# Loading the first token tile of x through two DMA queues in a one-core decoder-block kernel

## The chip, the cores and the metric

One core of a Trainium2 chip runs the whole kernel. The metric is the device time of one execution in microseconds (us). The engines named here are PE (TensorE, matrix products), ACT (ScalarE), DVE (VectorE), POOL (GpSimd) and SP (SyncE, which here only issues DMAs). Two engines issue DMAs in this kernel: SP on the queue that the profile calls q1, and ScalarE on the queue that it calls q10. "SPq" and "ACTq" are the instruction queues of those two engines.

## The reference, cut to what matters

```
ada = c @ w_ada + b_ada;  shift, scale, gate = split(ada, 3)
h   = rms_norm(x, g_pre) * (1 + scale) + shift        # x: 256 x 2048, float32
proj = h @ w_in                                       # then two attention branches,
...                                                   # their gates, a merge and w_out
x   = x + gate * rms_norm(y, g_post)
```

The change touches only the first lines: x and the small vectors (c, b_ada, g_pre, g_kv, g_subln) are read from HBM. Everything later is as it was.

## The kernel before, in words

x has 256 tokens, kept as two token tiles of 128 (one token to a partition) in `x_tok[:, t, :]`, 1 MB each. The matrix products want h with the model dimension on the partitions, so the opening turns x on PE. It also needs the modulation (shift and scale), which comes out of a product of the vector c with the first 4096 columns of w_ada. The opening goes so:

- **SP's queue.** L516 issues x tile 0, then tile 1, each with its own semaphore `x_in[t]`. Then L526 issues the sixteen halves of the first ada group (`load_ada(0, q)`, q from 0 to 7, 256 KB each, 4 MB in all) and L572 the first 512 KB weight piece (`w_raw`). After that weight pieces and later ada groups alternate in an order that is written out by hand.
- **ScalarE.** L971 and L974 issue five small DMAs that put the vectors into the rows of one tile, `vec_rows` (69 rows of 512 bytes), all on the semaphore `vec_in`. Then, per token tile, L979 squares x and sums it (waiting for `x_in[t]`). Then it copies the turned x out of PSUM (L983), casts the first weight piece (L1036) and makes the first h from turned x, gain and shift (L992). An activation table is loaded ahead of the first square.
- **POOL** makes the identity (L609, L611) and turns each sum of squares into 1/rms (L633, L636).
- **DVE** waits for the turned vectors, copies them out of PSUM into `cols` (L1541), makes small products of them (L1543, L1544, L1551), multiplies the identity by 1/rms of tile 0 (`make_diag(0)`, L1538), and then adds up the ada rows: two instructions for each q (L1435 for q = 0, L1438 after it), fifteen in all, since one of the sixteen parts is left to PE. `make_diag(1)` stands behind q = 1. At the end L1448 and L1449 make shift and gain for the first h.
- **PE** first runs four products whose results nobody reads (`keep_clock(6, 4)`, L1643). It waits for all five vector DMAs and turns `vec_rows` (L1814). It waits for `x_in[t]` and the diagonal of tile t and turns x in eight groups of four products, of which each shows as two instructions (L1823, 64 in all: groups 0 to 3 are tile 0, groups 4 to 7 are tile 1). After two more unread products (`keep_clock(1, 2)`) it sums the ada rows over the partitions in three sets (L1634): the odd rows, the part left to PE, the even rows. Then the first weight piece follows (L1899, L1913) and the stream of products that fills the rest of the kernel.

The order on each engine is the order in which its block is written, and each engine runs strictly by it; semaphores alone tie them together. A wait for one DMA is a wait for 16, since a DMA counts its semaphore up by 16.

Of the kernel before, what the change touches and what calls it, by code (L numbers as in the profile page):

```python
# [34 lines left out]
P = 128  # L35
D = 2048
SEQ = 256
TOK = SEQ // P
# [92 lines left out]
def hybrid_block(nc, x, c, positions, w_ada, b_ada, g_pre, w_in, g_kv, w_ukv,  # L131
# [78 lines left out]
    with ExitStack() as ctx:  # L210
# [8 lines left out]
        def sb(name, shape, dt, offset=None):  # L219
            size = 4 if dt != BF16 else 2  # L220
            for s in shape[1:]:
                size *= s
            if offset is None:
                offset = room((size + 31) // 32 * 32)
            return nc.alloc_sbuf_tensor_at(name, shape, dt, offset=offset)
# [22 lines left out]
        x_tok = sb("x_tok", [P, TOK, D], F32, r_o_lo)  # L248
# [96 lines left out]
        def sem(name):  # L345
            return ctx.enter_context(nc.semaphore(name))
# [5 lines left out]
        x_in = [sem(f"x_in{t}") for t in range(TOK)]  # L352
# [159 lines left out]

        @block.sync
        def _(sp):
            for t in range(TOK):
                sp.dma_start(x_tok[:, t, :], x[0, t * P:(t + 1) * P, :]).then_inc(x_in[t], 16)  # L516
            def load_ada(j, q):

                n = j * (KT // 2) + q
                if n >= ADA_RING:  # L520
                    sp.wait_ge(ada_used, n - ADA_RING + 1)
                if j == 1 and (q, 1) in FIRST_ON_PE:
                    sp.wait_ge(ada_direct, 1)
                for s in range(2):
                    col = s * D + j * 2 * P
                    sp.dma_start(ada_slot(n)[:, :, s, :],  # L526
                                 w_ada[0, 2 * q * P:2 * (q + 1) * P, col:col + 2 * P]
                                 .rearrange("(t p) n -> p t n", p=P)).then_inc(ada_in[n % ADA_RING], 16)
# [48 lines left out]
            for p, (a, kind, n, i, first, last) in enumerate(pieces):  # L577
# [18 lines left out]
                if kind == "wout" and n >= 1 and i % 2 == 0 and n < 3:  # L596
                    part = (n - 1) * 4 + i // 2
                    t, half = part // 4, slice(part % 4 * CH, (part % 4 + 1) * CH)
# [327 lines left out]
        for h in range(HEADS):  # L926
            s, t, v, g = mla_at[h]
# [3 lines left out]
            s, t, v, g = diff_at[h]  # L931
# [36 lines left out]

        @block.scalar
        def _(eng):  # L970
            eng.dma_start(vec_rows[V_C:V_C + KT, :], c[0, :].rearrange("(r n) -> r n", n=P)).then_inc(vec_in, 16)  # L971
            for row, n, v in ((V_SHIFT, 2 * KT, b_ada[0, 0:2 * D]), (V_GPRE, KT, g_pre[0, :]),
                              (V_GKV, RANK // P, g_kv[0, :]), (V_GSUB, 1, g_subln[0, :])):
                eng.dma_start(vec_rows[row:row + n, :], v.rearrange("(r n) -> r n", n=P)).then_inc(vec_in, 16)  # L974
            for t in range(TOK):
                eng.wait_ge(x_in[t], 16)
                if t:
                    eng.wait_ge(x_sq, t)
                act.activation(sq_junk[:, :], x_tok[:, t, :], ACT.Square, accum_out=sumsq[:, R_X, t:t + 1]).then_inc(x_sq, 1)  # L979
            for g in range(KT // 2):  # L980
                eng.wait_ge(xT_made, g + 1)
                t, k = g // 4, g % 4 * 4
# [388 lines left out]
        for h in range(HEADS):  # L1371
            s, t, v, g = mla_at[h]
# [4 lines left out]
            s, t, v, g = diff_at[h]  # L1377
            dve_after[g + 4].append(dve_o_lo(HEADS + h))
            dve_after[v + 4].append(head_squares(h))
        for h in range(HEADS):  # L1380
            s, t, v, g = diff_at[h]
# [229 lines left out]
        def _(pe):  # L1611
# [204 lines left out]
            for g in range(KT // 2):  # L1816
                t, k = g // 4, g % 4 * 4
                bank = g
                if g % 4 == 0:
                    pe.wait_ge(x_in[t], 16)  # L1820
                    pe.wait_ge(diag_ready, t + 1)
                for b in range(4):
                    ins = mm(ps[:, bank, b * P:(b + 1) * P], lhsT=x_tok[:, t, (k + b) * P:(k + b + 1) * P],  # L1823
                             rhs=x_diag[:, t, :], start=True, stop=True)
                ins.then_inc(xT_made, 1)
# [154 lines left out]
```

## Time and profile before

| | |
|---|---|
| median of three runs | 765.11 us (764.71 to 765.16) |
| the profiled execution, its own time | 764.76 us |
| its span in the trace | 763.0 us |
| PE busy in the span | 752.8 us |
| DVE, ACT busy | 560.3 us, 424.3 us |
| moved by DMA | 189.71 MB, mean 249 GB/s |

The span is what the trace records, from the first instruction to the last; the execution's own time is 1.8 us longer. A timeline row reads: start, duration, engine, line, operation, the tile written and the tile read, shapes, count, and in square brackets how long the engine was idle before and what ended that idle time. Consecutive instructions of one kind are merged into one row.

### The profile page before, as it was taken

How to read it: one execution, taken by the hardware profiler on the slowest of the kernel's cores; microseconds unless marked ns; L12 is line 12 of the kernel's file. 1: busy time of each engine (PE TensorE's matmuls, PEld its weight loads, DVE VectorE, ACT ScalarE, POOL GpSimd, SP SyncE). 2: the span in 40 equal slices, each digit the busy share in tenths (PEclk: the TensorE clock that was granted, in tenths of full speed). 3: DMA queues.
4: the chain of work that ended last, by engine and by line, in shares of the span. 5: the costliest groups of instructions: out<-in, count | busy, mean ns of one | idle time of the engine just before them, and what ended most of it. 6: DMA issues, size and time to landing. Idle time of an engine off the chain costs nothing.

```text
span 763.0 us, 10086 instructions
## 1 busy us (share of the span) xinstructions
PE 752.8 (99%) x3681; PEld 625.1 (82%) x3681; DVE 560.3 (73%) x823; ACT 424.3 (56%) x618; POOL 22.2 (3%) x95
## 2 busy tenths in 40 slices
PE   7999999999999999999999999999999999999997
PEld 5778888888888988888888888888888888888885
DVE  4899998888779579888987768776554556465554
ACT  5689777767656554544545664655444444444441
POOL 2000000000000000000000000011100000000001
PEclk9999999999999999999999999999999999999999
DMA  9999999999584788888886575555556656567642
GB/s 338 395 393 395 357 378 375 339 375 314 172 246 127 219 277 303 290 284 275 295 287 191 163 216 179 168 167 165 187 172 196 191 184 201 186 207 248 221 160 110
DMA packets 132555, 189.71 MB, mean 249 GB/s; under 512 B 10325, under 2 KB 68122, under 8 KB 132250
## 3 DMA queue, kind: packets, MB, share of 16 engines
q1 hardware_dynamic: 132240, 188.77, 74.0%
q8 instruction: 29, 0.48, 0.2%
q10 hardware_dynamic: 266, 0.30, 0.1%
q14 instruction: 20, 0.16, 0.1%
HBM read 185.90 MB, written 2.10 MB: 246 GB/s over the span
## 4 chain that ended last, share of the span: by engine, by line
PE 96%; SPq 2%; DMA 1%; ACT 1%; DVE 0%; issue 0%; DVEq 0%; ACTq 0%
PE ps L1923 17%; PE ps L1925 17%; PE ps L1924 17%; PE ps L1913 16%; PE ps L1899 8%; PE ps L1882 8%; PE ps L1885 4%; SPq L526 2%; PE ps L1718 1%; DMA w_raw<-in_w_in 1%; PE ps L1703 1%; PE ps L1733 1%; PE ps L1876 1%; PE ps L1875 1%; PE ps L1873 1%; PE ps L1692 0%
## 5 line engine op out<-in xcount | busy, mean ns | idle before, releaser
L1569 DVE TENSOR_TENSOR w_both<-w_raw,w_both 128x1024 fp32r<-128x1024 f32 x248 | 301.9, 1222 | 160.6 <-ACT w_both L1036 159.1
L1036 ACT CAST w_both<-w_raw 128x1024 fp32r<-128x1024 f32 x248 | 258.9, 1050 | 239.4 <-PE ps L1925 183.0
L1913 PE MATMUL ps<-w_both,h_both 128*128 128x512 f32 x560 | 138.5, 389 | 0.0
L1913 PEld LDWEIGHTS ps<-w_both,h_both 128*128 128x128 f32 x560 | 105.1, 188 | 22.2
L1923 PE MATMUL ps<-w_both,h_both 128*128 128x512 f32 x296 | 116.8, 395 | 0.0
L1925 PE MATMUL ps<-w_both,h_both 128*128 128x512 f32 x296 | 115.4, 390 | 0.0
L1924 PE MATMUL ps<-w_both,h_both 128*128 128x512 f32 x296 | 115.2, 389 | 0.0
L1899 PE MATMUL ps<-w_both,h_both 128*128 128x512 f32 x280 | 76.0, 393 | 1.0 <-ACT h_both L992 0.7
L1314 DVE SCALAR_TENSOR_TENSOR ada_acc<-ada_ring,cols,ada_acc 128x512 f32<-128x512 f32 x98 | 69.6, 745 | 0.5
L1923 PEld LDWEIGHTS ps<-w_both,h_both 128*128 128x128 f32 x296 | 55.6, 188 | 12.7 <-issue 1.7
L1925 PEld LDWEIGHTS ps<-w_both,h_both 128*128 128x128 f32 x296 | 55.6, 188 | 11.7
L1882 PE MATMUL ps<-h_both,w_both 128*128 128x512 f32 x256 | 64.9, 395 | 0.0
L1924 PEld LDWEIGHTS ps<-w_both,h_both 128*128 128x128 f32 x296 | 55.6, 188 | 11.0
L1899 PEld LDWEIGHTS ps<-w_both,h_both 128*128 128x128 f32 x280 | 51.7, 188 | 12.3 <-issue 1.0
L1882 PEld LDWEIGHTS ps<-h_both,w_both 128*128 128x128 f32 x256 | 46.1, 189 | 9.7 <-issue 1.3
L1923 PE MATMUL ps<-w_both,o_hi 128*128 128x512 f32 x128 | 50.2, 392 | 0.0
L1925 PE MATMUL ps<-w_both,o_lo 128*128 128x512 f32 x128 | 49.8, 389 | 0.0
L1924 PE MATMUL ps<-w_both,o_hi 128*128 128x512 f32 x128 | 49.8, 389 | 0.0
L1314 DVE SCALAR_TENSOR_TENSOR ada_acc<-gate_ring,cols,ada_acc 128x512 f32<-128x512 f32 x60 | 44.8, 747 | 2.1 <-DMA gate_ring<-in_w_ada 1.1
L1923 PE MATMUL ps<-w_both,m_hi 128*128 128x512 f32 x116 | 45.2, 390 | 0.0
L1925 PE MATMUL ps<-w_both,m_lo 128*128 128x512 f32 x116 | 45.2, 389 | 0.0
L1924 PE MATMUL ps<-w_both,m_hi 128*128 128x512 f32 x116 | 45.1, 389 | 0.0
(266 smaller groups left out, 849.3 us busy)
## 6 DMA issues: line engine op xcount, KB each, us to landing
w_raw<-in_w_in SPq DMA_DIRECT2D x177, 512.0 KB, 4.5
ada_ring<-in_w_ada SPq DMA_DIRECT2D x128, 256.0 KB, 6.8
gate_ring<-in_w_ada SPq DMA_DIRECT2D x32, 512.0 KB, 5.1
w_raw<-in_w_out SPq DMA_DIRECT2D x32, 512.0 KB, 3.8
w_raw<-in_w_o_mla SPq DMA_DIRECT2D x16, 512.0 KB, 3.7
w_raw<-in_w_o_diff SPq DMA_DIRECT2D x16, 512.0 KB, 4.1
w_raw<-in_w_ukv SPq DMA_DIRECT2D x16, 256.0 KB, 3.4
x_tok<-in_x SPq DMA_DIRECT2D x2, 1024.0 KB, 6.4
```

Of the source, the lines that this page charges most:

```text
L526: sp.dma_start(ada_slot(n)[:, :, s, :], w_ada[0, 2 * q * P:2 * (q + 1) * P, col:col + 2 * P] .rearrange("(t p) n -> p t n", p=P)).then_inc ...
L1036: act.copy(w_hi[:, p % RING, :], w_raw[:, p % RING, :]).then_inc(hi_done, 1)
L1314: ins = dve.scalar_tensor_tensor(out=acc, in0=src, scalar=cc, in1=acc, op0=ALU.mult, op1=ALU.add)
L1569: dve.tensor_tensor(w_lo[:, p % RING, :], w_raw[:, p % RING, :], w_hi[:, p % RING, :].bitcast(F32), ALU.subtract).then_inc(lo_done, 1)
L1703: mm(ps[:, 4 + w, lo:lo + keys], lhsT=qnT[:, 2 * u + w, t * P:(t + 1) * P], rhs=knT[:, 2 * u + w, 0:keys], start=t == 0, stop=False, skip_ ...
L1882: mm(ps[:, b0 + c, :], lhsT=w_hi[:, p % RING, (2 * r + c) * P:(2 * r + c + 1) * P], rhs=h_both[:, :, 4 * i + r, :], start=first and r == 0 ...
L1885: ins = mm(ps[:, b0 + c, 0:SEQ], lhsT=w_lo[:, p % RING, (2 * r + c) * P:(2 * r + c + 1) * P], rhs=h_hi[:, 4 * i + r, :], start=False, stop ...
L1899: mm(ps[:, b0 + t, :], lhsT=h_hi[:, 2 * i + r, t * P:(t + 1) * P], rhs=w_hi[:, p % RING, r * CH:(r + 1) * CH], start=fresh and r == 0, sto ...
L1913: ins = mm(ps[:, b0 + t, :], lhsT=side[:, 2 * i + r, t * P:(t + 1) * P], rhs=w[:, p % RING, r * CH:(r + 1) * CH], start=False, stop=last a ...
L1923: mm(o, lhsT=s_hi[:, k, q], rhs=hi, start=fresh and r == 0, stop=False, skip_group_check=kind == "early")
L1924: mm(o, lhsT=s_hi[:, k, q], rhs=lo, start=False, stop=False, skip_group_check=kind == "early")
L1925: ins = mm(o, lhsT=s_lo[:, k, q], rhs=hi, start=False, stop=last and r == tiles - 1, skip_group_check=kind == "early")
```

## The change

Tile 0 of x is loaded as two DMAs of 64 rows (512 KB each). Partitions 0 to 63 stay on SP's queue. Partitions 64 to 127 become the first DMA of ScalarE's queue, ahead of the five vector DMAs. Tile 1 stays on SP's queue, behind the first half of tile 0. The two places that wait for tile 0 (ScalarE's square and PE's turning) now wait for 32 on `x_in[0]`, and still for 16 on `x_in[1]`.

```diff
         @block.sync
         def _(sp):
-            for t in range(TOK):
-                sp.dma_start(x_tok[:, t, :], x[0, t * P:(t + 1) * P, :]).then_inc(x_in[t], 16)
+            sp.dma_start(x_tok[0:P // 2, 0, :], x[0, 0:P // 2, :]).then_inc(x_in[0], 16)
+            sp.dma_start(x_tok[:, 1, :], x[0, P:TOK * P, :]).then_inc(x_in[1], 16)
...
         @block.scalar
         def _(eng):
+            eng.dma_start(x_tok[P // 2:P, 0, :], x[0, P // 2:P, :]).then_inc(x_in[0], 16)
             eng.dma_start(vec_rows[V_C:V_C + KT, :], c[0, :].rearrange("(r n) -> r n", n=P)).then_inc(vec_in, 16)
...
             for t in range(TOK):
-                eng.wait_ge(x_in[t], 16)
+                eng.wait_ge(x_in[t], 16 * (2 - t))
...
                 if g % 4 == 0:
-                    pe.wait_ge(x_in[t], 16)
+                    pe.wait_ge(x_in[t], 16 * (2 - t))
                     pe.wait_ge(diag_ready, t + 1)
```

## Rows read from the trace of the kernel before

**Rows 1.** The page of the profile: span, PE's share, chain that ended last.

```profile
span 763.0 us, 10086 instructions
PE 752.8 (99%) x3681; PEld 625.1 (82%) x3681; DVE 560.3 (73%) x823; ACT 424.3 (56%) x618; POOL 22.2 (3%) x95
PE 96%; SPq 2%; DMA 1%; ACT 1%; DVE 0%; issue 0%; DVEq 0%; ACTq 0%
```

**Rows 2.** Waits of PE after the opening (24 to 764 us): total, times, longest.

```profile
PE ps L1954 <- ACT x_diag L1051: 1.1, 1, 1.1
PE ps L1899 <- ACT sum_junk L1005: 0.3, 1, 0.3
```

**Rows 3.** Timeline of PE's products, 1 to 24 us (start, duration, what).

```profile
1.51 5.60 PE L1643 MATMUL ps<-ident 128*128 128x512 f32 x8 [1.51 <-POOL ident L611]
8.57 0.25 PE L1814 MATMUL ps<-ident,vec_rows 69*128 69x69 f32 x1 [1.46 <-DMA vec_rows<-in_g_subln]
9.71 7.38 PE L1823 MATMUL ps<-x_diag,x_tok 128*128 128x128 f32 x64 [0.88 <-DVE x_diag L1538]
16.93 1.88 PE L1643 MATMUL ps<-ident 128*128 128x512 f32 x4
19.10 1.16 PE L1634 MATMUL ps<-ones,ada_acc 128*128 128x128 f32 x8 [0.29 <-DVE ada_acc L1438]
20.99 1.05 PE L1634 MATMUL ps<-ones,ada_acc 128*128 128x128 f32 x8
22.76 1.17 PE L1899 MATMUL ps<-w_both,h_both 128*128 128x512 f32 x4 [0.71 <-ACT h_both L992]
```

**Rows 4.** Timeline of the other engines, 0 to 32 us.

```profile
6.05 1.91 ACT L979 ACTIVATE sq_junk<-x_tok 128x2048 f32<-128x2048 f32 x1 [1.24 <-DMA x_tok<-in_x]
8.49 0.56 POOL L636 TENSOR_TENSOR rstd<-variance,power 128x1 f32<-128x1 f32 x1
8.65 1.91 ACT L979 ACTIVATE sq_junk<-x_tok 128x2048 f32<-128x2048 f32 x1 [0.60 <-DMA x_tok<-in_x]
...
8.86 0.23 DVE L1541 COPY cols<-ps 128x69 f32<-128x69 f32 x1 [8.86 <-PE ps L1814]
...
9.28 0.28 DVE L1538 TENSOR_SCALAR x_diag<-ident,rstd 128x128 f32<-128x128 f32 x1
9.48 0.17 DVE L1551 TENSOR_SCALAR cols<-cols 128x28 f32<-128x28 f32 x1
...
9.99 0.88 DVE L1435 TENSOR_SCALAR ada_acc<-ada_ring,cols 128x512 f32<-128x512 f32 x2 [0.34 <-DMA ada_ring<-in_w_ada]
...
11.40 1.45 DVE L1438 SCALAR_TENSOR_TENSOR ada_acc<-ada_ring,cols,ada_acc 128x512 f32<-128x512 f32 x2 [0.53 <-DMA ada_ring<-in_w_ada]
...
13.00 7.56 DVE L1438 SCALAR_TENSOR_TENSOR ada_acc<-ada_ring,cols,ada_acc 128x512 f32<-128x512 f32 x11
...
20.91 1.04 ACT L1036 CAST w_both<-w_raw 128x1024 fp32r<-128x1024 f32 x1 [3.19 <-DMA w_raw<-in_w_in]
...
22.01 1.09 ACT L992 ACTIVATE h_both<-xnT,mod_shift,mod_gain 128x256 fp32r<-128x256 f32 x2
```

**Rows 5.** The same timeline: issues on SPq and ACTq, and the table load.

```profile
0.72 0.86 SPq L516 DMA_DIRECT2D x_tok<-in_x  x2
...
2.11 1.13 ACTq L974 DMA_DIRECT2D vec_rows<-in_g_kv  x1
...
3.27 0.23 ACTq L974 DMA_DIRECT2D vec_rows<-in_g_subln  x1
...
3.53 1.28 ACT L979 ACT_TABLE_LOAD   x1 [3.53 <-issue]
```

**Rows 6.** DMA, 0 to 40 us: GB/s in each of 40 slices of 1 us.

```profile
GB/s 0 66 135 389 393 413 430 386 371 376 383 384 383 384 384 382 385 383 397 404 381 405 394 385 393 383 397 404 385 404 393 391 406 384 398 401 385 405 390 390
```

**Rows 7.** DMA, q10's packets at 0 to 4 us, then at 4 to 8 us.

```profile
q10 hardware_dynamic: 32, 0.01, 1.9%
...
q10 hardware_dynamic: 90, 0.03, 2.8%
```

**Rows 8.** Stretch 0 to 5 us: busy, PE clock, DMA share, GB/s (order of columns: PE PEld DVE ACT POOL).

```profile
0.00:5.00 5.00, 3.49 (x4) 1.50 (x5) 0.00 (x0) 1.28 (x1) 2.24 (x43) 1.00 0.54 197
```

## The prediction

> **What bounds the kernel now.** I began with the page. PE is busy for 752.8 of 763.0 us and the chain that ended last is 96% PE [rows 1]. So the end moves only by what moves PE's stream of products. The list of PE's waits after 24 us shows two: 0.3 us for the gain sums and 1.1 us for a diagonal at the very end [rows 2]. From the first product on a weight piece, at 22.76 us [rows 3], there is therefore next to nothing that could swallow a shift: whatever this change gains or loses, it gains or loses as a shift of that 22.76 us, about one for one. All that matters is what sets that moment.
>
> **What sets 22.76 us.** The timeline shows three paths that meet there, and the reader should see how near to each other they are.
>
> Path A, the weight piece. It lands just before the cast at 20.91 us; the cast ends at 21.95 and the first h starts at 22.01 [rows 4]. It is queued behind 2 MB of x and 4 MB of ada, and from 3 us on the DMA moves 370 to 430 GB/s without a gap [rows 6]. So path A is a matter of total bytes and of how early full rate is reached. ScalarE had idled 3.19 us ahead of the cast.
>
> Path B, the ada sums on DVE. It starts at 9.99 us, after 0.34 us of waiting for the first ada part, waits 0.53 us for the second, and from 13.00 us adds eleven times in 7.56 us, 0.69 us each, with no idle time of note [rows 4]. It lets PE start its three sets of sums at 19.10 us, after 0.29 us of idle time [rows 3].
>
> Path C, PE itself. It turns x from 9.71 us on, runs the unread products from 16.93 to 18.81, and from 19.10 the three sets of sums, of which the last ends at 22.04 (20.99 + 1.05) [rows 3]. Path C starts with the diagonal at 9.28 us, which stands on DVE behind the vector columns (8.86 us), which stand behind PE's turning of the vectors at 8.57, which waited 1.46 us for the last vector DMA [rows 3, 4].
>
> So paths B and C meet at PE's sums: B sets their start, and C has 0.29 us to spare against it. Path A meets them at the first h and has 0.06 us to spare, since the cast ends at 21.95.
>
> **The change, part by part.**
>
> Tile 0 of x. It must land before the square at 6.05 us [rows 4]. The same 1 MB goes over, now from two queues. Between 0 and 5 us the row of slices adds up to 66 + 135 + 389 + 393, or 0.98 MB [rows 6], about one tile, and the square starts a microsecond after that. At full rate one queue keeps the DMA engines busy, so a second queue can only help in the slow slices, 1 to 3 us. I take no gain. The bounds are 0 and the time that full rate in those two slices would give back: they moved 0.20 MB where 390 GB/s would have moved 0.78, so 0.58 MB or 1.5 us at most, and nothing suggests all of it. Even then the square's result is not what path C waits for: 1/rms of tile 0 is there at 9.05 (8.49 + 0.56), but DVE has the vector columns only at 9.09 (8.86 + 0.23) [rows 4]. An earlier tile 0 alone is worth nothing.
>
> That is the place to weigh a rule. The Trainium skill, page "DMA: Bandwidth & Descriptors", section "Rules for kernel authors", advises against two transfers to disjoint partition halves, because both halves run over the same 16 engines, whether issued from one engine or two. By it tile 0 lands when it did and the start stays. The trace bears it out above 3 us, where one queue already reaches 389 to 430 GB/s; for the two slow slices it shows only one queue.
>
> Tile 1 of x. On SP's queue it now has 0.5 MB ahead of it instead of 1 MB, but shares the engines with the half on ScalarE's queue. The sum of bytes until it is in is the same 2 MB, so it lands at 8.65 us as before [rows 4]. Its diagonal is made behind the second pair of ada rows, at about 12.8 us (just ahead of 13.00), long after. Nothing moves.
>
> The ada parts and the weight piece. They follow the same bytes in the same order, so paths A and B get their data when they did: 0, with the same ramp as the only upside. SP's issues: two DMAs before (0.86 us together [rows 5]), two after.
>
> The issue on ScalarE. One more DMA, 0.43 us (half of 0.86 [rows 5]), moves the five vector issues and the table load. The load ends at 4.81 us (3.53 + 1.28) and the square starts at 6.05 [rows 4, 5], so 1.24 us of idle time cover the 0.43. If the issue of g_kv, which took 1.13 us where its neighbour took 0.23 [rows 5], had a twin, 0.43 + 1.13 would overrun the cover by 0.3 us; 1/rms would be there at 9.4 instead of 9.05, which delays the diagonal by about 0.1 us. Path C hides that.
>
> The vectors, the one part that can hurt. Their last DMA now stands behind 0.5 MB on its own queue. Before, q10 had 32 packets in the first 4 us and 90 from 4 to 8 us, 122 in all [rows 7]; the first 32 found room between the packets of tile 0. Now those 32 come behind the half tile too, so about 122 have to pass in place of 90 once tile 0 is over at about 5 us. The last passed before 8 us, shortly before PE's start at 8.57 [rows 3]. If q10's packets keep taking turns with the large rows of x, 90 packets in the 2.7 us from 5.0 to 7.7 are 0.03 us each, and 32 more would cost 1.0 us; but tile 1 is over by about 7.7 us (2.1 MB by the slices of rows 6), and what takes turns with small ada packets goes fast. So the lower bound is 0, the upper 1.0 + 0.43 for the later issue, or 1.4 us, and I take 0.3 us, near the low end, since the large rows are gone for the last third. The vectors then turn at about 8.87 us, the diagonal moves from 9.28 to 9.58, PE's turning of x from 9.71 to 10.01 and the end of its unread products from 18.81 to 19.11, where the sums started at 19.10 anyway. DVE's ada rows could start at about 9.95 (9.48 + 0.17 + 0.3), still before the 9.99 at which their data comes. The loss is covered to within 0.02 us.
>
> **The sum.** Tile 0: 0. Tile 1: 0. Ada and weights: 0. Issue: 0. Vectors: 0.3 less 0.29 of cover, rounded up to 0.1 for the small delays that add to it. On the profiled execution's own 764.76 us that makes 764.9; that execution lies 0.35 us under the median of the three runs, so against the median 765.11 it is **765.2 us**.
>
> **The rivals.** In all of them, 0.2% of the time (1.5 us) is about the least that a measurement of this kernel can tell from no change.
>
> First rival: the ramp. Both queues start at 0.7 us, the slow slices fill, and all data comes 0.5 to 1.5 us sooner. For it: only 66 and 135 GB/s in those slices [rows 6]. Against a gain in time: path C does not hang on it. Paths A and B would come forward (B by up to 0.87 us, its two waits), but PE's turning and unread products end at 18.81 us, so the sums can begin 0.29 us sooner at best, and only if the vectors are no later. Time: 764.8 us. Still within 0.2%.
>
> Second rival: the vectors are late by the upper bound, 1.4 us, because ScalarE's queue gets fewer turns or its issues block. Path C then loses 1.4 - 0.29 = 1.1 us. Path B's columns are ready at 11.05 (9.65 + 1.4) in place of 9.65; its first pair then ends 0.5 us after the second ada part is there (11.05 + 0.88 against 11.40), and 0.5 is less than 1.1. Time: 766.2 us. It decides from 0.3 us of lateness on; for 0.2% it would need 1.8 us, beyond my bound.
>
> Third rival, the one on the slow side: PE's clock. The first eight unread instructions took 5.60 us, the later four of the same shape 1.88 us [rows 3]. At the later pace eight take 3.76, so the beginning, before PE had worked for some time, cost 1.84 us more. The granted clock reads 1.00 for that stretch too [rows 8], full speed (2.4 GHz), so the column doesn't show the slow pace; the durations do. Between 7.11 and 9.71 us PE does 0.25 us of work and yet turns x at the fast pace. A later vector DMA makes that pause longer (2.6 to 2.9 us by my term, up to 4.0 by its bound). If the slow pace comes back, turning x costs up to 1.84 us more, which goes straight into path C: 765.2 + 1.84, or 767.0 us. The point from which it decides is a pause that no row of this trace shows. Against it: the present 2.6 us did no harm, and I expect 0.3 more.
>
> Fourth: the change doesn't do what it says, that is, tile 0 is not sooner. That is my forecast already; its time is the same.
>
> **How the numbers follow.** Forecast 61%; the ramp (764.8) 15%; vectors late up to the bound (to 766.2) 13%; the clock (767.0) 4%; something that I don't see 7%, of which 4% faster and 3% slower by over 0.2%. The first three lie within 0.2%, so that is 89%; faster 4%; slower 4% + 3%. The range goes from the ramp's 764.8 less the spread of 0.4 us between the runs shown, 764.4, to the second rival's 766.2 and half of that spread, 766.4. Faster 0.04, within 0.2% 0.89, slower 0.07.
>
> **What would show it.** In the timeline of the changed kernel: the first square again near 6.0 us and the second near 8.6; the vectors turned at 8.6 to 9.2; the diagonal later by as much; the idle time of 0.29 us ahead of PE's sums shrunk to about nothing; the cast again at 20.9 and the first weight product at 22.7 to 22.9; 64 turning instructions again in about 7.4 us. In the slices of 1 us, tens of GB/s where 66 stood and less than 200 where 135 stood. The prediction is wrong if the vectors turn after 9.9 us, if the turning of x takes over 8 us, if the first weight product moves by more than 1 us either way, or if PE shows new waits after 24 us.

## The result and the profile after

The changed kernel takes 768.33 us (median of 6 runs, 767.8 to 769.09) against 764.98 us for the kernel before beside it (6 runs). The ratio is 1.0041, with a 95% interval of 1.003 to 1.0052: slower by 3.35 us. The forecast was 765.2 us, with a range to 766.4; the result lies above the range. The six executions fall into two groups: three take 767.80 to 767.92 us, with a granted clock of 0.996 to 0.998 on average, and three, the profiled one among them, take 768.73 to 769.09 us, with 0.994.

The page of the changed kernel, its lines that answer to [rows 1]:

```profile
span 767.1 us, 10087 instructions
PE 754.8 (98%) x3681; PEld 627.4 (82%) x3681; DVE 560.0 (73%) x823; ACT 423.6 (55%) x618; POOL 22.1 (3%) x95
...
PE 97%; DMA 1%; ACT 1%; DVE 0%; ACTq 0%; issue 0%; DVEq 0%
```

The span grew by 4.1 us (767.1 against 763.0), but PE's busy time by 2.0 us only; the profiled execution took 768.94 us, 0.6 us over the median. Where is the rest? The waits of PE behind 28 us answer that it is not in the long stream:

```profile
PE ps L1955 <- ACT x_diag L1052: 1.1, 1, 1.1
PE ps L1900 <- ACT sum_junk L1006: 0.4, 1, 0.4
```

They are those of [rows 2], within 0.1 us. So all of it must lie in the opening. PE's timeline, 1 to 28 us, to be held against [rows 3] (all lines of the changed kernel behind its new one on ScalarE are one higher):

```profile
1.51 6.19 PE L1644 MATMUL ps<-ident 128*128 128x512 f32 x8 [1.51 <-POOL ident L611]
11.56 0.35 PE L1815 MATMUL ps<-ident,vec_rows 69*128 69x69 f32 x1 [3.86 <-DMA vec_rows<-in_g_subln]
12.79 9.29 PE L1824 MATMUL ps<-x_diag,x_tok 128*128 128x128 f32 x64 [0.88 <-DVE x_diag L1539]
21.92 1.88 PE L1644 MATMUL ps<-ident 128*128 128x512 f32 x4
23.64 1.05 PE L1635 MATMUL ps<-ones,ada_acc 128*128 128x128 f32 x8
...
27.19 1.16 PE L1900 MATMUL ps<-w_both,h_both 128*128 128x512 f32 x4 [0.71 <-ACT h_both L993]
```

The first weight product stands at 27.19 us where it stood at 22.76: 4.43 us later, of which the stream behind it took up 0.3, since the span grew by 4.1. Two things are to be seen. The vectors turn 3.0 us later (11.56 against 8.57). And the 64 turning instructions of x take 9.29 us where they took 7.38. The idle time ahead of the sums is gone, as the prediction said it would be; the path through PE now decides.

The other engines, the same timeline, to be held against [rows 4]:

```profile
8.47 1.91 ACT L980 ACTIVATE sq_junk<-x_tok 128x2048 f32<-128x2048 f32 x1 [3.30 <-DMA x_tok<-in_x]
11.20 1.91 ACT L980 ACTIVATE sq_junk<-x_tok 128x2048 f32<-128x2048 f32 x1 [0.73 <-DMA x_tok<-in_x]
...
12.37 0.28 DVE L1539 TENSOR_SCALAR x_diag<-ident,rstd 128x128 f32<-128x128 f32 x1
...
13.77 1.45 DVE L1439 SCALAR_TENSOR_TENSOR ada_acc<-ada_ring,cols,ada_acc 128x512 f32<-128x512 f32 x2 [0.25 <-DMA ada_ring<-in_w_ada]
...
23.30 1.04 ACT L1037 CAST w_both<-w_raw 128x1024 fp32r<-128x1024 f32 x1 [0.59 <-DMA w_raw<-in_w_in]
```

Tile 0 is squared from 8.47 us on, 2.4 us later than before; tile 1 2.6 us, the second ada pair 2.4 us, the cast of the first weight piece 2.4 us later. So what comes by DMA on SP's queue is late by 2.4 to 2.6 us, and the vectors by 3.0. The slices of 1 us (as [rows 6]), and stretches with the columns of [rows 8], say why:

```profile
GB/s 0 0 270 221 238 221 201 168 355 373 354 384 385 379 389 380 385 385 381 385 386 402 394 390 406 382 379 395 381 409 380 389 393 377 398 383 380 398 375 389
```

```profile
3.00:4.00 1.00, 1.00 (x2) 0.34 (x1) 0.00 (x0) 0.12 (x1) 0.01 (x1) 1.00 0.97 221
4.00:5.00 1.00, 1.00 (x2) 0.34 (x1) 0.00 (x0) 1.00 (x1) 0.00 (x0) 1.00 1.05 238
...
3.00:7.00 4.00, 4.00 (x6) 1.54 (x5) 0.00 (x0) 1.28 (x1) 0.01 (x1) 1.00 1.04 220
7.00:8.00 1.00, 0.70 (x2) 0.00 (x0) 0.00 (x0) 0.00 (x0) 0.00 (x0) 1.00 0.91 168
...
10.00:14.00 4.00, 1.56 (x7) 1.42 (x8) 1.77 (x8) 2.48 (x4) 1.37 (x4) 0.50 1.06 376
14.00:18.00 4.00, 4.00 (x25) 4.00 (x25) 4.00 (x7) 1.52 (x3) 1.36 (x3) 0.65 1.09 385
```

From 2 to 8 us the DMA moves 168 to 270 GB/s where [rows 6] has 386 to 430 from 3 to 8 us. Yet the DMA share, the last column but one, is near 1: the 16 DMA engines are busy all the time, but each packet (one row of x, 8 KB) takes about twice as long. An estimate from the queue's packets and share in slices of 1 us: 0.62 us for a packet from 5 to 6 us here (27 packets, 104.1% of 16 engines), 0.31 us from 4 to 5 us in the kernel before (49 packets, 94.4%). And from 10 to 18 us the granted clock of PE is 0.50, then 0.65 on average: half speed (1.2 GHz) at first. Two queues, 2 to 4 us:

```profile
q10 hardware_dynamic: 60, 0.46, 97.7%
q1 hardware_dynamic: 4, 0.03, 5.9%
```

Although SP issued its half 0.01 us before ScalarE issued the other, ScalarE's half moved all but alone (60 packets to 4), and SP's followed it. The halves ran one after the other, not side by side.

### The profile page after: what moved, and what is told of

Read it like the earlier page. It is cut to its first block, busy times and chain, and to the rows that moved or that the text cites. A ratio compares the mean times of both kernels' runs of the same rounds, so it can differ in the third digit from the quotient of the medians.

```text
span 767.1 us, 10087 instructions
## 1 busy us (share of the span) xinstructions
PE 754.8 (98%) x3681; PEld 627.4 (82%) x3681; DVE 560.0 (73%) x823; ACT 423.6 (55%) x618; POOL 22.1 (3%) x95
## 4 chain that ended last, share of the span: by engine, by line
PE 97%; DMA 1%; ACT 1%; DVE 0%; ACTq 0%; issue 0%; DVEq 0%
PE ps L1924 17%; PE ps L1926 16%; PE ps L1925 16%; PE ps L1914 16%; PE ps L1900 8%; PE ps L1883 8%; PE ps L1886 4%; PE ps L1824 1%; DMA vec_rows<-in_g_subln 1%; PE ps L1719 1%; PE ps L1704 1%; PE ps L1734 1%; PE ps L1877 1%; PE ps L1876 0%; PE ps L1874 0%; PE ps L1693 0%
```

## The experiments

Three suspects come out of this: a DMA of half a tile moves at half the rate (or: two queues slow each other); the vectors stand behind x; PE's clock falls in the pause that results. First the four runs that part rows, queues and order. Each edit is against the changed kernel unless it says otherwise.

**The halves on one queue.**

```diff
             sp.dma_start(x_tok[0:P // 2, 0, :], x[0, 0:P // 2, :]).then_inc(x_in[0], 16)
+            sp.dma_start(x_tok[P // 2:P, 0, :], x[0, P // 2:P, :]).then_inc(x_in[0], 16)
...
-            eng.dma_start(x_tok[P // 2:P, 0, :], x[0, P // 2:P, :]).then_inc(x_in[0], 16)
```

> Both halves of tile 0 go over SP's queue, one behind the other; ScalarE's queue carries the vectors alone, as before. Theory H (a DMA that writes only 64 of the 128 partitions moves at half the rate, whatever queue it is on): the first square starts near 8.5 us as in the changed kernel, packets of the halves take about 0.65 us, the first 5 us move well under 300 GB/s; the vectors turn between 8.6 and 11 us. Time 766.5 to 768.5. Theory Q (it is the two queues together, with x on both, that slow each other): the first square is back near 6.0 us, the vectors at 8.5 us, time 765.

Measured: 767.74 us, ratio 1.0033 (1.002 to 1.0045). One stretch and the first square:

```profile
4.00:5.00 1.00, 1.00 (x3) 0.53 (x2) 0.00 (x0) 0.41 (x1) 0.00 (x0) 1.00 0.94 214
```

```profile
8.03 1.91 ACT L980 ACTIVATE sq_junk<-x_tok 128x2048 f32<-128x2048 f32 x1 [3.62 <-DMA x_tok<-in_x]
```

With a single queue the rate is as low. Theory Q falls. The vectors, alone on their queue, turn at 9.15 us, 2.4 us sooner than in the changed kernel, and the time is 0.6 us less: most of the loss does not hang on their place.

**Split by columns over both queues.**

```diff
-            sp.dma_start(x_tok[0:P // 2, 0, :], x[0, 0:P // 2, :]).then_inc(x_in[0], 16)
+            sp.dma_start(x_tok[:, 0, 0:D // 2], x[0, 0:P, 0:D // 2]).then_inc(x_in[0], 16)
...
-            eng.dma_start(x_tok[P // 2:P, 0, :], x[0, P // 2:P, :]).then_inc(x_in[0], 16)
+            eng.dma_start(x_tok[:, 0, D // 2:D], x[0, 0:P, D // 2:D]).then_inc(x_in[0], 16)
```

> Tile 0 is split over the two queues by columns instead of rows: 128 partitions times 4 KB on each. Same bytes and same order on each queue as in the changed kernel. Theory H: full rate from 3 us on, the first square near 6.0 us, the second near 8.6; the vectors still stand behind half a tile and turn at 8.6 to 9.5 us; time 765 to 766. Theory Q: the first square near 8.5 us again, the vectors at 11.5, time 768.

Measured: 765.26 us, ratio 1.0 (0.9991 to 1.0009).

```profile
2.00:3.00 1.00, 1.00 (x2) 0.35 (x2) 0.00 (x0) 0.00 (x0) 1.00 (x31) 1.00 0.62 152
3.00:4.00 1.00, 1.00 (x2) 0.34 (x1) 0.00 (x0) 0.03 (x1) 0.01 (x1) 1.00 1.03 414
```

```profile
5.78 1.91 ACT L980 ACTIVATE sq_junk<-x_tok 128x2048 f32<-128x2048 f32 x1 [0.52 <-DMA x_tok<-in_x]
8.64 0.25 PE L1815 MATMUL ps<-ident,vec_rows 69*128 69x69 f32 x1 [0.40 <-DMA vec_rows<-in_g_subln]
```

The same bytes, queues and order as in the changed kernel, with all 128 partitions in each DMA, and the loss is gone. The vectors, though behind half a tile, turn at 8.64 us, 0.07 us later than before. The slow start from 2 to 3 us is still there (152 GB/s): a second queue does not fill it.

**The whole tile on ScalarE's queue.**

```diff
-            sp.dma_start(x_tok[0:P // 2, 0, :], x[0, 0:P // 2, :]).then_inc(x_in[0], 16)
...
-            eng.dma_start(x_tok[P // 2:P, 0, :], x[0, P // 2:P, :]).then_inc(x_in[0], 16)
+            eng.dma_start(x_tok[:, 0, :], x[0, 0:P, :]).then_inc(x_in[0], 16)
...
-                eng.wait_ge(x_in[t], 16 * (2 - t))
+                eng.wait_ge(x_in[t], 16)
...
-                    pe.wait_ge(x_in[t], 16 * (2 - t))
+                    pe.wait_ge(x_in[t], 16)
```

> Tile 0 goes whole over ScalarE's queue ahead of the vectors, tile 1 over SP's. 128 partitions each. Theory H: nearly 400 GB/s from 3 us on; the two tiles take turns or follow each other, so the first square starts between 6.0 and 8.6 us and the vectors, behind 1 MB, turn at 8.6 to 9.5 us; time 765 to 766.5. Theory Q: below 300 GB/s while both are under way, the vectors at 11 us or later, time 768 or more.

Measured: 767.97 us, ratio 1.0039 (1.0026 to 1.0052). The rate is full (451 GB/s from 4 to 5 us), as H had it, but the time missed H's range.

```profile
8.47 1.91 ACT L979 ACTIVATE sq_junk<-x_tok 128x2048 f32<-128x2048 f32 x1 [3.48 <-DMA x_tok<-in_x]
10.57 1.91 ACT L979 ACTIVATE sq_junk<-x_tok 128x2048 f32<-128x2048 f32 x1
...
12.02 9.86 PE L1823 MATMUL ps<-x_diag,x_tok 128*128 128x128 f32 x64 [2.52 <-DVE x_diag L1538]
```

Both tiles take turns and land together (7.5 and 7.7 us after their issues), so tile 0 is 2.4 us late without any half rate, and x is turned in 9.86 us. This run shows a second way to lose the same time: the DMA that is wanted first, put beside one that is wanted later, got about every other turn (from 3 to 7 us 96 packets of ScalarE's queue to 99 of SP's). Its price cannot be read from the 768 us, since the slow clock is in them too: 9.86 us of turning is 2.5 us more than in [rows 3].

**The vectors first.**

```diff
-            eng.dma_start(x_tok[P // 2:P, 0, :], x[0, P // 2:P, :]).then_inc(x_in[0], 16)
             eng.dma_start(vec_rows[V_C:V_C + KT, :], c[0, :].rearrange("(r n) -> r n", n=P)).then_inc(vec_in, 16)
...
+            eng.dma_start(x_tok[P // 2:P, 0, :], x[0, P // 2:P, :]).then_inc(x_in[0], 16)
```

(The last line stands behind the loop over the vectors.)

> As the changed kernel, but the five vector DMAs are issued on ScalarE's queue ahead of the half tile. Theory H: the half tiles are still slow, so the first square starts at 8.5 to 10 us (its issue comes 2.5 us later); the vectors turn at 5 to 8 us; the diagonal now waits for 1/rms, at about 11.1 us or later. If PE's slow clock came only from the late vectors, the 64 turning instructions take 7.4 us here if PE's pause does not grow, and up to 9.3 if it does. Time 766.5 to 768.5. Theory V (the loss is that the vectors stand behind x, and little else): the vectors at 8.5 us or sooner, the diagonal at 9.3, time 765.

Measured: 771.0 us, ratio 1.0071 (1.0059 to 1.0084), above both ranges. The vectors turn at 8.23 us, but the square starts later still:

```profile
10.65 1.91 ACT L980 ACTIVATE sq_junk<-x_tok 128x2048 f32<-128x2048 f32 x1 [5.82 <-DMA x_tok<-in_x]
```

Issued 2.3 us later than in the changed kernel, the half tile moved only from about 8 to 10 us (195 GB/s), when SP's tile 1 was through. Theory V falls: to have the vectors early is worth nothing while tile 0 is late. The edit also makes tile 0 later still, so it does not price the place of the vectors; the first run of this section is the better test of it.

Next, the clock by itself, and rows once more.

**Clock held in the changed kernel.**

```diff
-            keep_clock(6, 4)
+            keep_clock(6, 8)
```

> The changed kernel with eight unread products ahead of the vectors in place of four, so that PE works until about 11.3 us and hardly pauses before the vectors turn. Nothing else moves. Theory K (part of the loss is PE's clock, which fell to half in the pause of 3.9 us): the granted clock stays 1.00 from 10 to 18 us, the 64 turning instructions take 7.4 us in place of 9.3, the first weight product comes at 25.2 us in place of 27.2, time 766.3 to 767. Rival (the turning is slow because tile 0 or the diagonal of tile 1 is late): the turning takes 9.3 us again and the time stays at 768.3.

Measured: 766.81 us, ratio 1.0023 (1.0014 to 1.0032).

```profile
12.15 7.38 PE L1824 MATMUL ps<-x_diag,x_tok 128*128 128x128 f32 x64 [0.88 <-DVE x_diag L1539]
```

```profile
12.00:14.00 2.00, 1.85 (x16) 1.88 (x17) 1.62 (x6) 1.42 (x3) 0.99 (x3) 1.00 1.09 383
```

The clock is 1.00, the turning takes 7.38 us as before, the first weight product stands at 24.65 us. Theory K stands: 1.5 us of the changed kernel's time is the clock (768.33 less 766.81). Of the 2.54 us between the first weight products of the two profiles the turning is 1.91; the rest is that the turning also began 0.64 us earlier (12.15 for 12.79), for which the edit gives no reason.

**No unread products in the kernel before** (its `keep_clock(6, 4)` taken out).

> The kernel before, without its first four unread products; loads as before. PE is idle until 8.5 us and begins to turn x at 9.7 us at half the clock. This measures the clock alone, with no DMA changed. Theory K: granted clock 0.50 at first, the 64 turning instructions take 9 to 11 us, the first weight product comes 1.4 to 3.3 us later than 22.76, time 766.5 to 768.5. Rival (the unread products do nothing for the time): 765.0.

Measured: 766.24 us, ratio 1.0012 (1.0004 to 1.0021). The loads are as before, the vectors turn at 8.52 us, but

```profile
9.78 9.15 PE L1822 MATMUL ps<-x_diag,x_tok 128*128 128x128 f32 x64 [0.91 <-DVE x_diag L1538]
```

takes 1.8 us more than in [rows 3], and the first weight product stands at 24.04 us. Theory K's direction holds and the size lies just below its range. The granted clock reads 1.00 in this whole stretch, against what K expected, though the products run slower than later ones of their shape; a slow beginning is to be read from durations.

**Rows interleaved.**

```diff
-            sp.dma_start(x_tok[0:P // 2, 0, :], x[0, 0:P // 2, :]).then_inc(x_in[0], 16)
+            sp.dma_start(x_tok[0:P:2, 0, :], x[0, 0:P:2, :]).then_inc(x_in[0], 16)
...
-            eng.dma_start(x_tok[P // 2:P, 0, :], x[0, P // 2:P, :]).then_inc(x_in[0], 16)
+            eng.dma_start(x_tok[1:P:2, 0, :], x[0, 1:P:2, :]).then_inc(x_in[0], 16)
```

> Tile 0 split by rows again, 64 rows on each queue, but even rows on SP's and odd rows on ScalarE's: each DMA has as many rows and bytes as in the changed kernel, spread over all 128 partitions. Theory P (a half is slow because its 64 neighbouring partitions are half of the ways into the tile): full rate from 3 us on, the first square near 6 us, time 765 to 765.7. Theory N (a DMA of 64 rows is slow whatever rows they are): packets near 0.65 us again, the first square at 8 to 8.5 us, time 768.

Measured: 765.5 us, ratio 1.0005 (0.9996 to 1.0014).

```profile
4.00:5.00 1.00, 1.00 (x2) 0.34 (x1) 0.00 (x0) 0.97 (x1) 0.00 (x0) 1.00 0.96 393
3.00:7.00 4.00, 4.00 (x7) 1.47 (x5) 0.00 (x0) 2.18 (x2) 0.01 (x1) 1.00 0.99 402
```

Its two queues, 2 to 4 us:

```profile
q10 hardware_dynamic: 64, 0.50, 70.2%
q1 hardware_dynamic: 3, 0.02, 3.0%
```

```profile
6.10 1.91 ACT L980 ACTIVATE sq_junk<-x_tok 128x2048 f32<-128x2048 f32 x1 [0.79 <-DMA x_tok<-in_x]
```

64 rows in each DMA, on two queues, at 393 GB/s. So it is neither the number of rows nor a split by rows, but that the 64 rows are neighbours. Nor is it the order: here too ScalarE's half went first, 64 packets to 3, and SP's behind it, at full rate. Theory P stands, with one thing that no run parts: a row of x in HBM is a partition of the tile, so blocks of neighbouring rows are neighbours on both sides of the DMA, and every other cut spreads both. That the limit is on the side of the partitions no run here shows. The Trainium skill says why, on the page "SBUF — State Buffer", section "Door 1: The DMA port swizzle": DMA bandwidth depends on how many of the 16 ports of the on-chip memory the partitions reach; partitions 0 to 63 are behind one eight of them, 64 to 127 behind the other eight. The traces agree with its consequence: from 3 to 7 us 220 GB/s for the halves, 402 for even and odd rows. The ports themselves are not in any trace here.

**Quarters on one queue.**

```diff
-            sp.dma_start(x_tok[0:P // 2, 0, :], x[0, 0:P // 2, :]).then_inc(x_in[0], 16)
+            for r in range(4):
+                sp.dma_start(x_tok[r * P // 4:(r + 1) * P // 4, 0, :], x[0, r * P // 4:(r + 1) * P // 4, :]).then_inc(x_in[0], 16)
...
-            eng.dma_start(x_tok[P // 2:P, 0, :], x[0, P // 2:P, :]).then_inc(x_in[0], 16)
...
-                eng.wait_ge(x_in[t], 16 * (2 - t))
+                eng.wait_ge(x_in[t], 16 * (4 - 3 * t))
```

(PE's wait likewise.)

> Tile 0 in four DMAs of 32 neighbouring rows each, all on SP's queue; the vectors alone on ScalarE's. It doubles the suspected cost. If the rate goes with the partitions that a DMA covers, a quarter moves at about 100 GB/s, so tile 0 takes about 10 us and the first square starts at 12.5 to 14 us; the first weight product near 29 us, time 771 to 774. If a DMA over fewer than 128 neighbouring partitions is simply limited to about 220 GB/s whatever its size, the first square starts near 8.1 us and the time is 767 to 768.

Measured: 767.58 us, ratio 1.003 (1.0019 to 1.0042).

```profile
4.00:5.00 1.00, 1.00 (x2) 0.34 (x1) 0.00 (x0) 0.27 (x1) 0.00 (x0) 1.00 0.94 215
```

```profile
7.57 1.91 ACT L980 ACTIVATE sq_junk<-x_tok 128x2048 f32<-128x2048 f32 x1 [3.29 <-DMA x_tok<-in_x]
```

215 GB/s, not 100: a quarter is no slower than a half. So the rate does not go with the number of partitions; the second branch of the expectation, about 220 GB/s whatever the size, holds. The same section of the Trainium skill says this too: a step of 32 partitions stays on the same port, so 32 neighbours reach the same eight ports as 64.

**Tile 1 in halves** (kernel before; tile 0 whole, tile 1 as two DMAs of 64 rows on SP's queue, the waits for tile 1 on 32).

> The kernel before, with tile 0 whole and tile 1 in two DMAs of 64 neighbouring rows, all on SP's queue. If the half rate belongs to the shape of the DMA and not to tile 0 or to the beginning, tile 0 is squared near 6.1 us as before, tile 1 lands 2 to 2.6 us later than 8.65, all ada parts and the weight piece come as much later, and the first weight product is at 24.5 to 26 us: time 766.5 to 768. If it belongs to the beginning (the engines' first packets), the time is 765.

Measured: 768.52 us, ratio 1.0039 (1.0026 to 1.0052).

```profile
4.00:5.00 1.00, 1.00 (x3) 0.42 (x2) 0.00 (x0) 0.47 (x1) 0.00 (x0) 1.00 0.98 410
...
7.00:8.00 1.00, 0.00 (x0) 0.00 (x0) 0.00 (x0) 0.98 (x1) 0.00 (x0) 1.00 0.91 207
```

Full rate while tile 0 moves, half of it while tile 1 does. It is the shape, wherever it stands. The time lies above the expected range. Tile 0 was squared at 7.02 us, later than expected, which stays open, and the vectors, alone on their queue, turned at 10.64 us; that their packets take turns with those of the halves, which last longer, is the likely reason, not a measured one. PE waited 3.84 us for them, and the turning of x took 8.91 us, so the slow clock is in this time too.

**Half rate alone.** Two runs have the halves on SP's queue, the vectors alone on ScalarE's (first edit of this section), and the clock held. The first had `keep_clock(6, 5)` and, behind `pe.wait_ge(cols_ready, 1)`, `keep_clock(6, 4)`:

> Both halves on SP's queue and the vectors alone on ScalarE's, as in the run of the halves on one queue, with five unread products before the vectors and four more behind them, so that PE has no pause over 1 us. What is left of the loss is the half rate alone. Expected: first square at 8.0 us, diagonal at 11.1, turning in 7.4 us, first weight product at 24.3 to 24.6 us, time 766.3 to 766.9 (1.1 to 1.7 us over the kernel before). If the first weight product is still at 25.6 us, the clock was not what made it late.

Measured: 767.76 us, ratio 1.0037 (1.0025 to 1.005). It missed: the four products behind the vectors ran from 10.20 to 13.90 us, past the diagonal at 11.23, and held up the turning themselves. The second had 7 and 1:

> The halves on SP's queue once more, the vectors alone on ScalarE's, with seven unread products ahead of the vectors and one behind them. In the last such run the four behind them took 3.7 us and ended 2.1 us after they could, so PE turned x late by their own length. Here they should end by 11.6 us, with the diagonal. Expected: granted clock 1.00 throughout, turning from 11.6 us in 7.4 us, first weight product at 24.4 us, time 766.5 to 766.9. At 767.7 again the rest of the loss would lie elsewhere than in the clock and in the time at which the data comes.

Measured: 766.64 us, ratio 1.0018 (1.0009 to 1.0027).

```profile
11.57 7.38 PE L1825 MATMUL ps<-x_diag,x_tok 128*128 128x128 f32 x64 [0.34 <-DVE x_diag L1539]
...
24.29 1.17 PE L1901 MATMUL ps<-w_both,h_both 128*128 128x512 f32 x4 [0.71 <-ACT h_both L993]
```

With the clock held and the vectors off the path (the diagonal, at 11.14 us, waits for 1/rms of tile 0), this is the price of the half rate: 1.57 us (766.64 less 765.07 beside it).

**Another order for tile 1** (kernel before; tile 1 issued behind `load_ada(0, 1)`), a try for something better.

> The kernel before, with tile 1 of x issued behind the first two ada parts instead of ahead of them. The ada parts then land 2.6 us sooner, DVE starts its rows at 9.7 us without the two waits (0.87 us in all), while tile 1 lands at about 11.3 us and its diagonal is made some 0.5 us later than before, at 13.5 to 14 us. The first weight product is bound by PE (0.29 us to gain) and by the weight piece, which keeps its place in the bytes: 22.5 to 23.2 us, time 764.8 to 765.5, no difference that can be measured.

Measured: 766.37 us, ratio 1.0017 (1.0008 to 1.0026): slower, a miss.

```profile
14.48 0.30 DVE L1539 TENSOR_SCALAR x_diag<-ident,rstd 128x128 f32<-128x128 f32 x1 [2.85 <-POOL rstd L637]
14.70 7.61 DVE L1439 SCALAR_TENSOR_TENSOR ada_acc<-ada_ring,cols,ada_acc 128x512 f32<-128x512 f32 x11
14.93 3.81 PE L1824 MATMUL ps<-x_diag,x_tok 128*128 128x128 f32 x32 [1.54 <-DVE x_diag L1539]
```

DVE reached the diagonal of tile 1 early and stood still 2.85 us for it, with its eleven ada additions behind. They began at 14.70 us instead of 13.00. I had counted when the diagonal would come and not what is queued behind it. No run here was faster than the kernel before.

## Why the prediction was wrong, point by point

**What holds.** The end moves with the first weight product, roughly one for one: its shifts of +0.5 (columns), +1.5 (half rate alone), +1.9 (clock held), +4.4 us (changed) stand beside +0.2, +1.9, +2.0 and +4.1 us in the spans of the same executions, and +0.0, +1.6, +1.7 and +3.4 us in the medians. The changed kernel's profiled execution took 768.94 us, 0.6 over its median, hence its larger shift. The 0.29 us of idle time ahead of the sums is gone, and PE shows no new wait behind the opening.

**The step that failed** is "Tile 0 of x": "At full rate one queue keeps the DMA engines busy, so a second queue can only help". I took 0, with a gain as the other bound, and excluded a loss on the ground that the bytes are the same. The bytes were the same and the rate was not: a DMA into 64 neighbouring partitions moves at about half of it (220 against 406 GB/s from 3 to 7 us). Tile 0 came 2.4 us late, and with the same argument, the same bytes in the same order, I had put tile 1, ada and the weight piece at 0, where they too came 2.4 to 2.6 us late. No row of the kernel before showed the rate of a DMA over 64 partitions. The rule of the Trainium skill, as I weighed it there, forecast no gain, and I read no loss in it; its reason, that both halves use the same 16 engines, fits the trace (one half alone kept them 97.7% busy from 2 to 4 us) and does not bear on the rate.

**The vectors.** I took 0.3 us, bound 1.4; they turned 3.0 us later. The term itself, vectors behind half a tile on their queue, was well sized: with the half tile cut by columns it is 0.07 us. With half rate the same place makes them much later: 11.02 us in the changed kernel with its clock held, 9.53 with the vectors alone on their queue. Of these 1.5 us 0.9 were covered, since with the vectors alone the diagonal waits for 1/rms: it came 0.59 us later (11.73 for 11.14), and the medians differ by 0.14 us (1.71 less 1.57 over the kernel before), less than the spread of 0.4 to 0.5 us within either run. So it takes both, the place behind the half tile and the half rate, to make 3 us. That the vectors' small packets have to pass between large ones that last twice as long is the likely way, argued and not measured.

**The clock.** The third rival was right in kind: 1.84 us expected, 1.91 us measured in the turning (9.29 less 7.38), 1.5 us between the medians of the changed kernel with and without the clock held (768.33 and 766.81). That the price agrees so closely is in part luck: over the six profiles in which the column shows 0.50 the turning took 8.87 to 10.16 us, that is 1.5 to 2.8 us more, and the first eight unread instructions, from which I had taken the 1.84, took 5.18 to 6.72 us in profiles of kernels that leave them alone. Its chance of 4% was wrong because I let the pause grow by my own 0.3 us. PE paused from 7.70 to 11.56 us, 3.9 us, then worked 0.35 us and paused 0.9 us more; the granted clock fell to 0.50 in this pause (0.99 from 9 to 10 us, 0.50 from 10 to 12). It is an effect of the other two and not a cause by itself.

**The sum as measured:** half rate 1.57, the vectors' place 0.14, the clock 1.64 (3.35 less 1.71), together 3.35 us, in place of my 0.1. These are differences of one kernel to the next, so they add up by the way they are made; the first and the last are clear of the noise, the middle one is not.

## What to carry to other kernels

Cut a transfer so that every piece spans all 128 partitions: by columns, or by rows with a stride, never into blocks of neighbouring partitions; the same bytes on the same queues took 765.3, 765.5 and 768.3 us. Neither good cut was faster than the whole tile on one queue. When a change delays the first work of PE, ask what the longer pause does to its clock before you price the rest. And a bound of "no loss, since the bytes are the same" needs a row that shows the rate of that very shape.

## What the runs showed of the hardware that I had not expected

- From 3 to 7 us, with the DMA engines shown as busy, the six kernels that load tile 0 in blocks of 64 or 32 neighbouring rows, with tile 1 behind them, move 218 to 231 GB/s. With tile 1 behind or beside a tile 0 that is whole, or cut into column halves or interleaved rows, it is 399 to 426.
- Two halves of 64 rows issued 0.01 us apart on two queues ran one after the other, ScalarE's first, whether the rows were neighbours (60 packets to 4 from 2 to 4 us) or interleaved (64 to 3), while two whole tiles (32 to 28) and two column halves (62 to 76) took turns. In the run with the vectors first, too, ScalarE's half moved only when SP's tile 1 was through. So it goes with the DMA of 64 rows and not with the rate; why stays open.
- The slow packets reach a little into tile 1, whole as it is: 168 GB/s from 7 to 8 us in the changed kernel, 263 with the same loads in the clock-held run, 322 with the halves on one queue. No run was made for it.
- The granted clock reads 1.00 from the start of every trace, also where products of the same shape take longer than later on.
